# Reordering a mixture-of-experts chunk: the combine step between the two up-projections, the transpose inside the light expert's product

## The reference

```python
def swiglu(x, w1, w3, w2):
    return (jax.nn.silu(x @ w1) * (x @ w3)) @ w2

def moe_ffn(xn, router_w, router_b, w1, w3, w2):
    logits = (xn @ router_w).astype(jnp.float32) + router_b.astype(jnp.float32)
    top_v, top_i = lax.top_k(logits, TOP_K)
    w = jax.nn.softmax(top_v, axis=-1)
    gate = jnp.sum(jax.nn.one_hot(top_i, N_EXPERTS, dtype=jnp.float32) * w[..., None], axis=-2)
    out = jnp.zeros_like(xn)
    for e in range(N_EXPERTS):
        out = out + gate[..., e:e + 1] * swiglu(xn, w1[e], w3[e], w2[e])
    return out
```

## Time and profile before

| | before |
|---|---|
| median of 3 runs | 1674.63 us |
| the profiled execution | 1675.24 us |
| its span | 1673.3 us |
| TensorE busy | 1655.7 us, 99% |
| VectorE busy | 1069.5 us, 64% |
| ScalarE busy | 877.2 us, 52% |
| HBM read | 483.15 MB, 289 GB/s over the span |

### The profile page before, as it was taken

How to read it: one execution, slowest core, us unless ns; L and a number is a source line. 1 busy time by engine, 2 the same in 40 slices (tenths; PEclk the granted TensorE clock), 3 DMA queues, 4 the chain that set the end, 5 groups by cost and what they waited for, 6 DMA issues and landing times.

```text
span 1673.3 us, 25482 instructions
## 1 busy us (share of the span) xinstructions
PE 1655.7 (99%) x10246; PEld 1299.5 (78%) x10246; DVE 1069.5 (64%) x1662; ACT 877.2 (52%) x1349; POOL 20.0 (1%) x51
## 2 busy tenths in 40 slices
PE   9999999999999999998999999999999999999998
PEld 8888999999999988996666666666656666566667
DVE  7697876665678897866554555644646446455456
ACT  6778644433456778635444544544545446354444
POOL 4000000000000000000000000000000000000000
PEclk9999999999999999998999999999999999999999
DMA  8342453643454443446999999999999999999980
GB/s 337 148 164 102 165 220 144 242 170 152 182 189 162 174 149 117 152 158 251 378 424 413 403 420 416 424 423 394 421 414 421 426 393 423 422 415 424 393 362 28
DMA packets 38124, 485.94 MB, mean 290 GB/s; under 512 B 4192, under 2 KB 6512, under 8 KB 8816
## 3 DMA queue, kind: packets, MB, share of 16 engines
q1 hardware_dynamic: 37824, 484.08, 71.4%
q10 hardware_dynamic: 176, 0.15, 0.0%
HBM read 483.15 MB, written 1.07 MB: 289 GB/s over the span
## 4 chain that ended last, share of the span: by engine, by line
PE 96%; DVE 2%; ACT 1%; DMA 0%; issue 0%; POOL 0%; DVEq 0%; POOLq 0%
PE work L1179 17%; PE work L1180 16%; PE work L1181 16%; PE acc L1527 12%; PE acc L1181 6%; PE acc L1179 6%; PE acc L1552 6%; PE acc L1180 6%; PE acc L1260 1%; PE pv_ps L1490 1%; PE misc L1444 1%; PE misc L1446 1%; PE misc L1428 1%; PE acc L1298 1%; PE misc L1437 1%; PE misc L1542 1%
## 5 line engine op out<-in xcount | busy, mean ns | idle before, releaser
L489 DVE TENSOR_TENSOR w_lo<-raw,w_hi 128x1024 fp32r<-128x1024 f32 x236 | 283.9, 1219 | 84.8 <-ACT w_hi L484 83.1
L1179 PE MATMUL work<-x_r,w_hi 128*128 128x256 f32 x1024 | 296.9, 290 | 0.8 <-DVE gate_b L1976 0.7
L1181 PE MATMUL work<-x_r,w_lo 128*128 128x256 f32 x1024 | 289.6, 283 | 0.0
L1180 PE MATMUL work<-x_r,w_hi 128*128 128x256 f32 x1024 | 289.5, 283 | 0.0
L484 ACT ACTIVATE w_hi<-raw 128x1024 fp32r<-128x1024 f32 x236 | 241.8, 1048 | 66.2 <-PE acc L1181 29.1
L2214 DVE TENSOR_TENSOR w_lo<-raw,w_hi 128x1024 fp32r<-128x1024 f32 x208 | 241.2, 1219 | 30.3 <-ACT w_hi L1008 30.3
L1008 ACT ACTIVATE w_hi<-raw 128x1024 fp32r<-128x1024 f32 x208 | 206.8, 1052 | 95.1 <-DMA raw<-in_moe_w 79.1
L1179 PEld LDWEIGHTS work<-x_r,w_hi 128*128 128x128 f32 x1024 | 196.0, 191 | 8.7 <-issue 6.2
L1180 PEld LDWEIGHTS work<-x_r,w_hi 128*128 128x128 f32 x1024 | 196.1, 192 | 1.0 <-issue 0.7
L1181 PEld LDWEIGHTS work<-x_r,w_lo 128*128 128x128 f32 x1024 | 196.1, 191 | 0.0
L1179 PE MATMUL work<-w_hi,bias_r 128*128 128x512 f32 x448 | 178.7, 399 | 2.7 <-DVE w_lo L2214 2.7
(11 more groups left out here) (356 smaller groups left out, 3234.4 us busy)
## 6 DMA issues: line engine op xcount, KB each, us to landing
raw<-in_moe_w SPq DMA_DIRECT2D x102, 2048.0 KB, 13.1
raw<-in_mix_w SPq DMA_DIRECT2D x33, 2048.0 KB, 8.1
spare<-in_moe_w SPq DMA_DIRECT2D x33, 2048.0 KB, 13.2
x<-in_moe_w SPq DMA_DIRECT2D x33, 2048.0 KB, 12.9
raw<-in_dense_w SPq DMA_DIRECT2D x21, 2048.0 KB, 8.2
raw<-in_ple_w SPq DMA_DIRECT2D x4, 2048.0 KB, 9.5
raw<-in_mix_w SPq DMA_DIRECT2D x4, 512.0 KB, 6.7
spare<-in_ple_p SPq DMA_DIRECT2D x2, 1024.0 KB, 10.2
```

What stands on the lines that cost most here:

```text
L489: eng.tensor_tensor(unit(w_lo, g), raw_part(g), unit(w_hi, g).bitcast(F32), ALU.subtract).then_inc(split_ok, 1)
L1179: pe.matmul(out, stat[0], move[0], start=start, stop=False, skip_group_check=True)
L1180: pe.matmul(out, stat[0], move[1], start=False, stop=False, skip_group_check=True)
L1181: return pe.matmul(out, stat[1], move[0], start=False, stop=stop, skip_group_check=True)
```

## The change

Nothing is added or taken away: the same instructions run in another order, on three engines.

- TensorE: `between` moves from behind `turn` to between the two halves of `up`. `turn` moves from behind k = 7 of `up_light` to behind k = 1. `turn_light` comes after two quarters of `down` instead of three.
- ScalarE: `silu` comes after six splits of the pass instead of eight, `stage_gathered` and `stage_gathered_light` come ahead of `turned_hi`, `turned_hi` ahead of the splits 8 and 9, and `next_tokens` ahead of the splits 10 and 11.
- VectorE: `add_combined` comes ahead of `hidden`, `turned_lo` ahead of the splits 8 and 9, `next_tokens_lo` ahead of the splits 10 and 11.

```diff
--- before.py
+++ after.py
@@ -1060,30 +1060,31 @@
                         hi_m("couple", i, n + q)
                     if c == 0:
                         take_y("couple", i)
-                    for q in range(4, 8):
+                    for q in range(4, 6):
                         hi_m("couple", i, n + q)
                     silu("couple", i, c)
+                    for q in range(6, 8):
+                        hi_m("couple", i, n + q)
                     if c == 0:
                         light_tokens(i)
                     if c == 4:
+                        stage_gathered_light(i)
                         take_gates("couple", i)
+                    if c >= 5:
+                        stage_gathered(i, c - 5)
+                    turned_hi("couple", i, c)
                     for q in range(8, 10):
                         hi_m("couple", i, n + q)
-                    turned_hi("couple", i, c)
 
                     ge(act, l_used, "couple", i, LIGHT_N, 0, LIGHT_C * c + 3)
                     act.activation(l_both, quad[2], ACT.Copy).then_inc(l_both_ok, 1)
+                    if c == FC - 1:
+                        next_tokens(i)
                     for q in range(10, 12):
                         hi_m("couple", i, n + q)
-                    if c == 4:
-                        stage_gathered_light(i)
-                    if c >= 5:
-                        stage_gathered(i, c - 5)
                     ge(act, l_turned, "couple", i, FC, 0, c + 1)
                     act.activation(l_gate, misc[:, :].rearrange("p (f n) -> p f n", f=FT)[:, :, 0:LIGHT],
                                    ACT.Silu).then_inc(l_silu_ok, 1)
-                    if c == FC - 1:
-                        next_tokens(i)
 
             def extra(r):
                 for c in range(FC):
@@ -1570,16 +1571,17 @@
             def couple(i):
                 for c in range(FC):
                     up("couple", i, 0, c)
+                    between(i, c)
                     up("couple", i, 1, c)
                     if c == 4:
                         turn_gates("couple", i)
                     for k in range(KT):
                         up_light(i, c, k)
-                    turn("couple", i, c)
-                    between(i, c)
+                        if k == 1:
+                            turn("couple", i, c)
                     for ft in range(FT):
                         down("couple", i, c, ft)
-                        if ft == 2:
+                        if ft == 1:
                             turn_light(i, c)
                     for ft in range(FT):
                         down_light(i, c, ft)
@@ -2229,19 +2231,19 @@
                     n = HEAVY_C * c
                     for q in range(8):
                         lo_m("couple", i, n + q)
+                    if c < 4:
+                        add_combined("couple", i, c)
                     hidden("couple", i, c)
+                    turned_lo("couple", i, c)
                     for q in range(8, 10):
                         lo_m("couple", i, n + q)
-                    turned_lo("couple", i, c)
-                    if c < 4:
-                        add_combined("couple", i, c)
+                    if c == FC - 1:
+                        next_tokens_lo(i)
                     for q in range(10, 12):
                         lo_m("couple", i, n + q)
                     ge(dve, l_silu_ok, "couple", i, FC, 0, c + 1)
                     dve.tensor_tensor(l_hid, l_gate, misc[:, :].rearrange("p (f n) -> p f n", f=FT)[:, :, LIGHT:P],
                                       ALU.mult).then_inc(l_hid_ok, 1)
-                    if c == FC - 1:
-                        next_tokens_lo(i)
                     if c == 1:
                         build_pick(rank_m, bass.ds(i * 2 + 2, 1))
                         build_light_pick(bass.ds(i * 2 + 3, 1))
```

## The result

The changed kernel takes 1688.78 us (median of 6 runs, 1687.19 to 1689.47), the kernel before in the same sessions 1674.93 us (1674.51 to 1676.22). The ratio is 1.0079, 95% interval 1.0067 to 1.0090: 13.9 us slower. The forecast was 1688.6 us; single runs of either kernel lie up to 2.3 us apart, so that a hit within 0.2 us is partly luck.

What follows compares the result with a forecast made beforehand. TensorE, not the loads, was taken to bound the stage. Borders 10.4, waits 3.4 and the end 0.2 sum to 14.0 us: 1674.6 + 14.0 = 1688.6 us, forecast 1685 to 1693, 8-in-10 range 1678 to 1697.

Steps and rivals of the forecast that it cites:

- parts 1 and 2: TensorE's added border costs in every pass, narrow tile and combine row together: 0.37 us a pass, 10.4 us in all.
- part 3: Late inputs of TensorE: next_tokens delays quarter 10 by 0.85 us in four passes c = 6, 3.4 us; other waits covered.
- cover of quarter 10: In down, starting at E, quarter 10 is ready at E + 2.9 and wanted at E + 3.2: 0.3 us left.
- part 4: Loads on SP's queue: slots come free later, but the longer period affords the idle DMA; costed at 0.
- part 5: End of the mixture: the next stage's weights land later, delaying take_y's last copy by 0 to 0.7 us, taken as 0.2.
- Part 1: TensorE enters and leaves the 64-wide tile three times a pass instead of twice: 0.34 us a pass.
- Part 2: The combine row between the halves of up changes TensorE's borders: 0.03 us a pass, ends 0 and 0.1.
- The upper bound of part 1: 0.34 + 0.16 us a pass, if down paid both the narrow block's border and the step behind a combine row.
- the thin cover: Quarter 10's 0.3 us in down; the rival has it break in all 28 passes, 1694 to 1700 us, chance 0.12.
- Free borders: Rival: TensorE's borders cost nothing or are made up for, only late inputs remain, 1675 to 1678 us; chance 0.11.
- loads as the bound: Rival: a pass's transfers could take 31 us and set the pace, 28 us more, 1703 us; chance 0.06.
- transposes beside the light matmuls: Rival: turn overlaps the light matmuls on TensorE, saving 0.5 us and its borders each pass, 1664 us; chance 0.06.

Runs made afterwards that it cites:

- `turn` in two pieces: The changed kernel with two of the four transposes behind k = 1 and two behind k = 3 of up_light: 1697.18 us, ratio 1.0131.
- `turn` alone: The kernel before with one edit, turn moved behind k = 1 of up_light: 1685.14 us, ratio 1.0060.
- The test that used the cover up: The changed kernel with turn_light back behind three quarters of down instead of two: 1696.72 us, ratio 1.0132.
- the combine step alone: The kernel before with one edit, the combine step (between) moved between the halves of up: 1723.70 us, ratio 1.0291.
- the fast kernel: The kernel before with down_light directly ahead of the next pass's up_light, light gate and light hidden tile behind that pass's fourth split: 1663.52 us, ratio 0.9934.
- both slow experiments: The kernel before with between moved between up's halves, 1723.70 us; the kernel before with down_light moved ahead of the next up_light, light gate unmoved, 1718.84 us.

## Why the prediction was right, step by step

| step | predicted | measured |
|---|---|---|
| parts 1 and 2, a usual pass | + 0.37 us | + 0.367 us |
| part 3, four waits in c = 6 | 0.85 us each | 0.84, 0.80, 0.80 for the three whose pass can be measured |
| part 3, cover of quarter 10 | 0.3 us | `w_lo` ready 0.29 us ahead |
| part 3, quarters 6 and 7 ready in the pass | 8.6 and 9.7 us | 8.57 and 9.70 us |
| part 4, loads | 0 | no wait of TensorE |
| part 5, last copy | 0.2 us | 0: the wait of 0.7 us is that of before |
| sum on the profiled execution | 14.0 us | 13.3 us |

**What bounds.** The claim that TensorE sets the pace though the DMA share reads 1.00 is shown from both sides: with TensorE's sequence longer the loads slowed to 413 GB/s, with it shorter they rose to 426. The share of 1.00 was no limit yet at 419 GB/s.

**Part 1** is shown. One, two, three and four narrow blocks a pass make passes of 29.59, 29.98, 30.35 and 30.66 us: 0.39, 0.37 and 0.31 a block. They differ with what stands behind the added block's end: the way in costs 0.09, the first pair 0.05 and the end of the block 0.10 in each case, and the first step behind it 0.11 more where it is a split matmul (the changed kernel, 0.34 instead of 0.23) and 0.06 where it is a transpose (`turn` in two pieces, 0.17 instead of 0.11). Narrow instructions in the same place pay no border: both their own steps and those of the light matmuls round them are at the pace of the stream. The Trainium skill ("TensorEngine Tiling (Array Packing)", Key Properties) has a change of the tiling mode drain the engine, and all four agree with it; the size is these runs'.

**Part 2** is sized well too, 0.01 us against the 0.03 forecast: the combine row and its border take the same 1.96 us wherever they stand, and `turn` alone (30.353 us) makes the whole of the changed kernel's pass (30.347). Part 1 then is 0.36 instead of 0.34. The upper bound of part 1, in which `down` pays both for the narrow block and 0.16 behind a combine row, didn't come: its first step is 0.34.

**Part 3** is shown by taking the copies out of the way, and the thin cover by using it up. The cover in the changed kernel, in the pass shown above:

```profile
1076.99 2.36 DVE L2216 TENSOR_TENSOR w_lo<-x,w_hi 128x1024 fp32r<-128x1024 f32 x2 [2.96 <-ACT w_hi L1008]
1078.50 0.48 PE L1180 MATMUL acc<-w_hi,bias_r 128*128 128x512 f32 x1
```

The first of the two takes 1.22 us and is done at 1078.21, 0.29 ahead of the matmul. `down` starts at 1075.29, so this is 2.92 behind it, where the prediction has E + 2.9, and the matmul 3.21, where it has E + 3.2. The test that used the cover up also shows a term that the prediction lacked, the 0.11 us of restart behind a wait. It didn't matter for the forecast, because the first split matmul behind `turn_light` has a long step anyway: 0.32 us without a wait (1078.50 to 1078.82), 0.34 with it.

**The 0.7 us** by which 14.0 was too much is the balance of several things. The mixture became 12.7 us longer, and the largest part of what is missing there is the first pass: it takes 31.90 us against 32.28, though a usual one is 0.37 longer. The granted clock there is at 0.50, the 1.2 GHz level, for the first microseconds, and the stretch ended sooner: from 780 to 782 us the clock reads 0.58 in the kernel before and 0.94 in the changed one. TensorE had sat idle for 2.73 and 2.44 us just ahead, and I know of no cause in the change. The surplus of the first pass over a usual one is 2.30 us in the kernel before and 1.55 in the changed kernel and with `turn` alone, but 2.45 with the combine step alone and 2.2 in the changed kernel with `turn_light` back: it goes with neither order. The four waits are 0.05 us shorter than forecast, and the last copy costs nothing. Against that the stretch behind the mixture was 44.7 us in this profile and 44.3 before, which the prediction had not; the profiles of the other runs have 44.2 to 44.4, so that it is no effect of the new order. So the first pass, the tail and the rest met by luck; the 0.37 a pass and the 0.8 in c = 6 did not.

**The rivals.** Free borders fell with the run of `turn` alone, the thin cover holds by 0.29 us in the changed kernel, loads as the bound fell since TensorE has no wait for a load in the changed kernel, and with the fast kernel's 426 GB/s, and transposes beside the light matmuls, the rival on the other side, are refuted by 0.59 us for four of them.

## What to carry to other kernels

When an engine is full and the profile names no wait, read the distances from start to start at the borders between kinds of instruction: what is lost there is in no view of waits, and grouping the 64-wide matmuls into fewer blocks was worth 0.3 to 0.4 us a block. Before moving work on the bounding engine, list what each moved piece covered, for the other engines' in-order lists: both slow experiments here (48 and 43 us) took away a cover of 1.6 to 3.6 us that no busy share shows. A DMA share of 1.00 did not mean here that loads were the limit; that was told by who waits for them.

## What the runs showed of the hardware that I had not expected

- A wait of 0.12 us costs 0.23: the first split matmul behind it needs 0.34 us instead of 0.23 to the next, as it does behind a change of width, and as it does behind the wait of 1.58 us. Waits below about 0.16 us, the 0.39 of a record less the 0.23 of a step, don't show in the waits view, since the modelled end of the matmul before covers them.
- The DMA share read 1.00 at 412 and at 419 GB/s and 1.01 at 426 GB/s, so that it isn't a measure of what is left.
- A long first step isn't always a price. Behind a combine row the first split matmul needs 0.39 to 0.42 us instead of 0.23, but the row's last records are short by as much, and the sum is a hundredth. Behind a narrow block nothing makes up for the long step: 0.34 for a split matmul, and 0.54 instead of 0.43 for a plain fp32 one.
